# Two transformer blocks in one launch: another order for the passes of half the rows, the hyena's steps, norm and the bias loads

## The reference, cut to what matters

```python
logits = einsum('bqhd,bsd->bqhs', qib, k_idx32) * idx_scale      # 16 heads of 64; 2 blocks of 128 queries
score = einsum('bqhs,bqh->bqs', relu(logits), wb)                # then the 64 best keys of each query
...
h = h @ w4                                    # filter taps: 256 positions, 64 hidden, 2 x 1024 channels
h_fwd, h_bwd = h[:, :1024] * decay, h[:, 1024:] * decay
k = concatenate([h_fwd, zeros, h_bwd[:0:-1]])
k = k / sum(abs(k), axis=0)                   # "norm" in the kernel
...
z = hv * x1
z = bidir_fft_conv(z, filt) + hy_bias * z     # spectra of z and of the filter, product, back
y_h = z * x0
...
g_h, g_a = split(sigmoid(g + b_gate), 2)      # 8 groups of 512 columns
```

## Time and profile before

| | |
|---|---|
| median of 3 runs | 2093.49 us (2090.84 to 2102.37) |
| profiled execution | 2100.09 us, span 2098.3 us |
| mean granted clock of TensorE | 0.985 |
| TensorE busy | 97% |
| VectorE busy | 63% |
| ScalarE busy | 44% |
| DMA | 194 GB/s over the span |

### The profile page before, as it was taken

How to read it: one execution, slowest core, us unless ns; L and a number is a source line. 1 busy time by engine, 2 the same in 40 slices (tenths; PEclk the granted TensorE clock), 3 DMA queues, 4 the chain that set the end, 5 groups by cost and what they waited for, 6 DMA issues and landing times.

```text
span 2098.3 us, 23578 instructions
## 1 busy us (share of the span) xinstructions
PE 2043.2 (97%) x9229; PEld 1614.4 (77%) x9229; DVE 1317.6 (63%) x1675; ACT 927.6 (44%) x1226; POOL 382.9 (18%) x588
## 2 busy tenths in 40 slices
PE   6989999999999999999899999999999999999999
PEld 1268787777887888787688888888888888878887
DVE  4867667789676678867975665554444544444443
ACT  1165523455654544344454434454444444443342
POOL 0000001999999960000000000000000000000000
PEclk9999989999999999999999999999999999999999
DMA  9967656555566675544345555555555555656554
GB/s 351 331 246 240 212 185 207 189 177 161 178 199 196 197 228 180 178 142 157 124 150 177 198 186 179 184 195 184 197 181 195 185 193 188 198 163 200 189 192 160
DMA packets 206243, 407.94 MB, mean 194 GB/s; under 512 B 10874, under 2 KB 12979, under 8 KB 205491
## 3 DMA queue, kind: packets, MB, share of 16 engines
q1 hardware_dynamic: 190480, 376.07, 54.1%
q10 hardware_dynamic: 13892, 23.88, 3.4%
q0 software_dynamic: 1760, 6.49, 1.5%
HBM read 404.31 MB, written 2.10 MB: 194 GB/s over the span
## 4 chain that ended last, share of the span: by engine, by line
PE 88%; DVE 7%; DMA 3%; issue 1%; ACT 1%; ACTq 0%; SPq 0%; DVEq 0%
PE ps L430 80%; PE pm L511 5%; DMA raw<-in_ada_w 2%; DVE raw_lo L408 2%; PE ps L511 1%; PE pm L523 1%; DVE mod_part L1148 1%; DMA raw<-in_w_in 1%; PE pm L575 0%; PE pm L885 0%; DVE xtmp L1348 0%; DVE sc_i L1265 0%; DMA gate<-in_b_gate 0%; DVE xtmp L1546 0%; DMA rows_b<-in_hgrn_norm_g 0%
## 5 line engine op out<-in xcount | busy, mean ns | idle before, releaser
L408 DVE TENSOR_TENSOR raw_lo<-raw,w_hi 128x1024 fp32r<-128x1024 f32 (+1 forms) x648 | 799.5, 1237 | 580.0 <-ACT w_hi L399 570.6
L399 ACT ACTIVATE w_hi<-raw 128x1024 fp32r<-128x1024 f32 (+1 forms) x648 | 680.1, 1051 | 809.4 <-PE ps L430 783.5
L430 PE MATMUL ps<-w_hi,h_hi 128*128 128x512 f32 (+1 forms) x2336 | 943.8, 404 | 19.7 <-DVE raw_lo L408 13.5
L430 PE MATMUL ps<-w_hi,h_lo 128*128 128x512 f32 (+1 forms) x2336 | 915.1, 392 | 0.0
L430 PE MATMUL ps<-raw_lo,h_hi 128*128 128x512 f32 (+1 forms) x2336 | 914.7, 392 | 0.0
L430 PEld LDWEIGHTS ps<-w_hi,h_hi 128*128 128x128 f32 x2336 | 444.1, 190 | 126.6 <-DVE raw_lo L408 20.7
L430 PEld LDWEIGHTS ps<-raw_lo,h_hi 128*128 128x128 f32 x2336 | 444.6, 190 | 93.1 <-issue 7.4
L430 PEld LDWEIGHTS ps<-w_hi,h_lo 128*128 128x128 f32 x2336 | 443.8, 190 | 93.7
L2305 POOL TENSOR_TENSOR proj<-proj 128x128 f32<-128x128 f32 x264 | 177.0, 675 | 12.9
L2305 POOL TENSOR_TENSOR proj<-proj,w1T 128x128 f32<-128x128 f32 x165 | 102.3, 628 | 11.3 <-DMA proj<-in_z 4.1
L430 PE MATMUL ps<-w_hi,hid_hi 128*128 128x512 f32 x256 | 100.0, 391 | 2.0 <-DVE raw_lo L408 2.0
(11 more groups left out here) (320 smaller groups left out, 1168.0 us busy)
## 6 DMA issues: line engine op xcount, KB each, us to landing
raw<-in_w_in SPq DMA_DIRECT2D x140, 1024.0 KB, 5.3
raw<-in_w_ffn_gate SPq DMA_DIRECT2D x44, 1024.0 KB, 5.1
raw<-in_w_ffn_up SPq DMA_DIRECT2D x44, 1024.0 KB, 5.1
raw<-in_w_ffn_down SPq DMA_DIRECT2D x44, 1024.0 KB, 5.1
raw<-in_ada_w SPq DMA_DIRECT2D x32, 1024.0 KB, 7.7
raw<-in_w_out SPq DMA_DIRECT2D x32, 1024.0 KB, 5.2
proj<-in_ada_w ACTq DMA_DIRECT2D x16, 1024.0 KB, 5.2
raw<-in_w_br_hyena SPq DMA_DIRECT2D x8, 1024.0 KB, 5.2
```

The costliest lines, as they stand in the source:

```text
L399: nc.scalar.activation(w_hi[:, p % HRING, :, 0:gm.width(j)], raw[:, k % RING, e:e + HT, 0:gm.width(j)], ACT.Copy).then_inc(hi_done, 1)
L408: nc.vector.tensor_tensor(raw_lo[:, k % RING, e:e + HT, 0:gm.width(j)], raw[:, k % RING, e:e + HT, 0:gm.width(j)], w_hi[:, p % HRING, :, 0 ...
L430: mm = nc.tensor.matmul(ps[pair][:, t, 0:gm.width(j)], l[:, tok], r[:, i, 0:gm.width(j)], start=(k == 0 and q == 0), stop=(k == kt - 1 and ...
```

## The change

Index: the steps j and j+1 are done together at the part of the even one, in two banks, and the products alternate between the row halves. Taps: two units at a time, products alternate between row halves and banks. Norm: DVE adds `decay[:, 1]` to `decay[:, 0]` first, and TensorE does one product per block of channels. z's spectrum: the second four units are two parts later; DVE's twelve steps are done at most one a part (in parts 81, 83, and 84 to 93); the convolutions start at part 97. Bias: slot 0 is loaded after the weight loads of group 9, slot 1 after those of group 10.

```diff
@@ -96,7 +96,7 @@
 SPEC_AT = 69
 Z_AT = 56
 ZSPEC_AT = 77
-CONV_AT = 92
+CONV_AT = 97
 ROTATE_AT = 72
 QK2_AT = 86
 AT2_AT = 93
@@ -656,15 +656,17 @@
                 i.then_inc(filled, 1)
                 for t in range(TT):
                     nk = P * (t + 1)
-                    for j in range(IDX_H // 2):
+                    for j in range(0, IDX_H // 2, 2):
                         yield INDEX_AT[1 + t] + j
                         if t == 0 and j == 0:
                             drained(("ki", 0))
-                        b = bank(pe, ("ix", t, j), "a")
-                        part = slice(IDX_D * (j % 2), IDX_D * (j % 2) + IDX_D)
+                        b = [bank(pe, ("ix", t, j + r), "a") for r in range(2)]
                         for q in range(2):
-                            m = mm(b[:, q * SEQ:q * SEQ + nk], qiT[part, j // 2 * 2 + q, t * P:t * P + P], kiT[part, 0:nk])
-                        m.then_inc(filled, 1)
+                            for r in range(2):
+                                part = slice(IDX_D * r, IDX_D * r + IDX_D)
+                                m = mm(b[r][:, q * SEQ:q * SEQ + nk], qiT[part, j + q, t * P:t * P + P], kiT[part, 0:nk])
+                                if q:
+                                    m.then_inc(filled, 1)
 
             def gate_rows():
                 for j in range(ADA_GATE):
@@ -752,24 +754,23 @@
                     yield i2(LAYER_AT[n])
                     pe.wait_ge(sig(f"sin{n + 1}"), 1)
                     mm(bank(pe, ("layer", n), "v")[:, 0:P], w23[:, n], h3T[:]).then_inc(filled, 1)
-                for i in range(4 * TT):
-                    yield i2(TAPS_AT + i // 2)
-                    if i == 0:
+                for n in range(4):
+                    yield i2(TAPS_AT + n)
+                    if n == 0:
                         pe.wait_ge(sig("w4_in"), 16 * TT)
                         pe.wait_ge(sig("sin3"), 1)
-                    odd, n = i % TT, i // TT
-                    b = bank(pe, ("taps", odd, n), "v")
-                    for t in range(TT):
+                    b = [bank(pe, ("taps", odd, n), "v") for odd in range(2)]
+                    for odd, t in ((1, 0), (0, 1), (0, 0), (1, 1)):
                         part = slice(HID * t, HID * t + HID)
-                        m = mm(b[P // 2 * t:P // 2 * t + P // 2, :], h3T[part, :].rearrange("p (m s) -> p s m", s=2)[:, odd],
+                        m = mm(b[odd][P // 2 * t:P // 2 * t + P // 2, :], h3T[part, :].rearrange("p (m s) -> p s m", s=2)[:, odd],
                                w4[part, n * GW:n * GW + GW], skip_group_check=True)
-                    m.then_inc(filled, 1)
+                        if (odd, t) in ((0, 0), (1, 1)):
+                            m.then_inc(filled, 1)
                 yield i2(NORM_AT)
                 pe.wait_ge(sig("abs_ready"), 1)
                 b = bank(pe, "norm", "v")
                 for c in range(8):
-                    for t in range(TT):
-                        m = mm(b[:, c:c + 1], decay[:, t, c * P:c * P + P], ones[:, 0:1], start=(t == 0), stop=(t == TT - 1))
+                    m = mm(b[:, c:c + 1], decay[:, 0, c * P:c * P + P], ones[:, 0:1])
                 m.then_inc(filled, 1)
                 for i in range(8):
                     yield i2(SPEC_AT + i)
@@ -796,7 +797,7 @@
                             m = nc.tensor.transpose(b[:, c * P:c * P + P], y_t[4 * u + c].rearrange("p (m s) -> p s m", s=2)[:, t], ident[:])
                         m.then_inc(filled, 1)
                 for i in range(8):
-                    yield i2(ZSPEC_AT + i)
+                    yield i2(ZSPEC_AT + i + 2 * (i // 4))
                     drained(("z", 1, 1))
                     n, j, odd = i // 4, i // 2 % 2, i % 2
                     mm(bank(pe, ("zspec", n, j, odd), "v" if odd else "a")[:, :], dft[:, j, odd, 0:P],
@@ -1480,6 +1481,7 @@
                     yield i2(ABS_AT + 3 * t + 2)
                     link(v.tensor_tensor(decay[:, t], decay[:, t], w4v[:, t], ALU.add))
                     yield i2(ABS_AT + 3 * t + 3)
+                link(v.tensor_tensor(decay[:, 0], decay[:, 0], decay[:, 1], ALU.add))
                 dve.sem_inc(sig("abs_ready"), 1)
                 for t in range(TT):
                     link(v.tensor_tensor(w4v[:, t], hf[:, t], hb[:, t], ALU.subtract))
@@ -1562,10 +1564,10 @@
                         dve.sem_inc(sig("y_spec"), 1)
 
                 for at, step in ((1, lambda: slots(("zspec", 0, 0), hf, 0, 0)), (3, lambda: slots(("zspec", 0, 1), hb, 0, 1)),
-                                 (4, lambda: slot_product(0, 0)), (5, lambda: slots(("zspec", 1, 0), hf, 1, 0)),
-                                 (5, lambda: slot_product(0, 1)), (6, lambda: parities(0, 0)), (7, lambda: slots(("zspec", 1, 1), hb, 1, 1)),
-                                 (7, lambda: parities(0, 1)), (8, lambda: slot_product(1, 0)), (9, lambda: slot_product(1, 1)),
-                                 (10, lambda: parities(1, 0)), (11, lambda: parities(1, 1))):
+                                 (4, lambda: slot_product(0, 0)), (5, lambda: slot_product(0, 1)), (6, lambda: parities(0, 0)),
+                                 (7, lambda: slots(("zspec", 1, 0), hf, 1, 0)), (8, lambda: parities(0, 1)),
+                                 (9, lambda: slots(("zspec", 1, 1), hb, 1, 1)), (10, lambda: slot_product(1, 0)),
+                                 (11, lambda: slot_product(1, 1)), (12, lambda: parities(1, 0)), (13, lambda: parities(1, 1))):
                     yield i2(ZSPEC_AT + at + LEAD)
                     step()
                 for c in range(8):
@@ -2125,7 +2127,7 @@
                         turned_by(("x0", 3))
                         s.activation(z_tok[:, t, u * GW:u * GW + GW], b[:, :], ACT.Copy).then_inc(used["a"], 1)
                 for i in range(4):
-                    yield i2(ZSPEC_AT + 2 * i + LEAD)
+                    yield i2(ZSPEC_AT + 2 * i + 2 * (i // 2) + LEAD)
                     n, j = i // 2, i % 2
                     b = content(act, ("zspec", n, j, 0), "a")
                     s.activation((hf, hb)[j][:, 0, n * GW:n * GW + GW], b[:, :], ACT.Copy).then_inc(used["a"], 1)
@@ -2252,7 +2254,7 @@
 
             def beside_i2(j):
 
-                for g in (0, 1) if j == I2_G + 1 else (j - I2_G,) if j > I2_G + 1 else ():
+                for g in (j - I2_G,) if j >= I2_G else ():
                     if g >= 2:
                         evacuated(sp, g_i2, j - 2)
                     else:
```

## The result

The changed kernel takes 2082.76 us (median of 18 runs, 2080.76 to 2090.40); the kernel before, run beside it, 2096.81 (18 runs). The ratio is 0.9933, with a 95% interval of 0.9923 to 0.9943: faster by some 14 us, 0.67%. The forecast was a gain of 12.5 us and 2081.0 us. The profiled execution has a span of 2080.8 us and a mean granted clock of 0.987.

What follows compares the result with a forecast made beforehand. TensorE, busy 97% of the span, was taken as the bound. Index -2.0, taps 0, norm -3.5, convolutions 0, bias and steps -7.0 sum to -12.5 us: 2081.0 us on the median, range 2074 to 2090.

Steps and rivals of the forecast that it cites:

- Bound: Whole kernel: TensorE busy for 97% of the span, so edits pay by removing its instructions, waits or slow stretches.
- Index, -2.0 us: Paired index steps: passes overlap, relieving TensorE of 8.6 us, but VectorE covers them; 2.6 us gained, 0.6 off for slow clock.
- Taps, 0: Taps products alternating over row halves and banks: they overlap already, so no gain; range +1 to -4 us.
- Rival D: Taps: row halves in one bank wait for each other today, so separate banks save 3.9 us; 2077.1 us, chance 0.04.
- Norm, -3.5 us: Norm: 16 passes instead of 32 save 1.8 us, plus half of the 3.4 us lost to slow clock behind them.
- Bias and steps, -7.0 us: Hyena's steps: the bias stall goes and low halves come earlier; 7.8 us gained, 0.8 off for slow clock.
- Convolutions with attention, 0: Six parts instead of one fill all four banks: no cost entered, up to +6 us.
- Rival C: Parts 99 to 104: TensorE waits for readers of all four banks, costing 15 us; 2096 us, chance 0.06.
- The sum: All terms together: 12.5 us gained, giving 2081.0 us on the median.
- rival B: Waits in parts 86, 87 and before part 100 bring slow clock, norm's slow stretch stays: +6.8 us, 2087.8 us, chance 0.27.

Runs made afterwards that it cites:

- norm_only: The kernel before with the norm edit alone (added sum, one product per block): 2091.82 us, ratio 0.9987.
- bias_only: The kernel before with only the bias loads moved: 2089.05 us, ratio 0.9983.
- steps_only: The kernel before with only the later second spectrum units, VectorE's new list of steps and convolutions from part 97: 2090.46 us, ratio 0.9981.
- steps_wide: The changed kernel with the hyena's steps spread wider (VectorE's in parts 81 to 97) and convolutions from part 101: 2082.09 us, ratio to before 0.9939.
- q_later: The changed kernel with the second attention's transposes of q two parts later and of k one part later: 2084.59 us, ratio to before 0.9959.
- search_late: The changed kernel with the second row block's search for the 64 best keys one round a part from two parts later: 2085.40 us.
- index_only: The kernel before with the paired index steps alone: 2093.21 us, ratio 1.0001.
- both_moved: The changed kernel with the edits of both search_late and steps_wide: 2081.11 us, ratio to before 0.9935.
- both_mended: both_moved with convolutions from part 97 again and the first sine layer two parts later: 2076.94 us, ratio to before 0.9908.
- in_turn: The changed kernel with both index products of the lower row half issued first, still in two banks: 2089.76 us in one execution.
- norot pair: The kernel before without the first attention's rotations on VectorE, once with the index as before (2091.10 us), once with the index edit (2084.50 us).
- norot_single: The kernel before without the first attention's rotations on VectorE, index as before: 2091.10 us, ratio 0.9980.

## Why the prediction was right, and where it was off

**Bound.** Right: the gain is instructions and slow clock of TensorE, and the waits for low halves stayed at 14.6 us.

**Index, -2.0 us.** The mechanism held in each step: passes of 0.72 and 1.14 us, a wait near 452 us, VectorE as the cover (8.5 us arrive without its rotations), a gain that is VectorE's alone. The size was too large: 1.0 us in the trace of the changed kernel, 1.2 in that of the edit alone, nothing that shows in its ratio. Two terms were mis-sized. VectorE's starts came 2.0 us earlier, not 2.6. And I wrote off 0.6 us for slow clock, with the new wait before part 100 as its likely cause; it was a second one, the 3.04 us before 506.65, that had the slow stretch behind it, some 1.1 us lost (clock 0.91 over 500 to 520). I had taken the existing wait of 1.63 us there as something that stays as it is; it became 1.28 and 3.04, since TensorE arrived earlier and VectorE hardly did. That is the forecast's own rule, that an earlier TensorE waits longer, not carried to the end of the stretch.

**Taps, 0.** Right: eight passes in 1.94 us before and after the earlier trace rows. The rule of the Trainium skill that was weighed there (TensorEngine Tiling (Array Packing), Gotcha 1: PSUM Pressure) doesn't show where the halves write to different partitions of a bank: giving them a bank each changed nothing. Rival D has fallen.

**Norm, -3.5 us.** Too small: 5.0 us in the trace, close to the upper end of its range, 5.2. The 1.8 us of passes were right; the slow stretch behind them, of which I had taken half, went altogether (1.00 where 0.79 stood), in the changed kernel and in norm_only. bias_only keeps the 32 passes and had them in 3.62 us instead of 4.51, with a granted clock of 0.89 over the 16 us from their start, and gains 1.6 us on the kernel before there without any edit of norm: against that execution sixteen passes are worth 3.4 us. How much is slow varies from one execution to the next; that no slow stretch follows sixteen did not, in eight.

**Bias and steps, -7.0 us.** Right: 7.6, or 6.6 to 7.1 without what was chance in the execution before. The stall went, and the low halves of parts 83 to 93 came in the forecast's order. TensorE was to be idle for 5.3 us in pieces of 1.0 to 1.5; it was 4.3 in pieces of 0.96, 0.76, 1.35 and 1.22, two of them ahead of q's transposes as I had said (1.0 and 1.5), and the clock stayed at 1.00. That neither edit alone does it, and that about half comes from each, is what bias_only and steps_only add.

**Convolutions with attention, 0.** Right: TensorE busy for 70.00 of 70.00 us. Rival C didn't come, though steps_wide shows its mechanism in one part, 99, when the convolutions start four parts later still.

**The sum.** Two errors of opposite sign, index 1.0 too large and norm 1.5 too small, met, so 12.5 stood against 13.6 in the traces and 14.0 in the medians; that they nearly cancelled is luck. The time, 2082.76, lies 1.8 us above 2081.0: the kernel before took 2096.81 in the longer set of runs instead of 2093.49, 3.3 us more, and the gain was 1.5 us larger. None of rival B's slow stretches came in the changed kernel's trace; the one behind the wait near part 100 came in four other kernels (below). B was weighed by two waits, 1.63 us without a slow stretch and 3.75 with one. The same trace of before had more to weigh it by: a wait of 1.87 us at 1026 us and one of 2.22 at 641 were each followed by a slow stretch, one of 1.99 at 1851 was not.

## What to carry to other kernels

Count the work that an edit takes off the busiest engine, and then look for the engine that is ready just in time beside it: the index edit relieved TensorE of 8.5 us and brought about 1, because VectorE was busy 96% of the stretch. Where a second engine is without a pause, change its work or its order; and when that pays, look further down the program for the engine that the gain does not reach (GpSimd's filter sum here) and for the place whose cover was moved. Where VectorE set the pace, two waits of TensorE that were taken away came back as one longer one (q_later), with the same idle time in all and a slow stretch behind it.

## What the runs showed of the hardware that was not expected

**The same wait has two prices.** All kernels with the paired index passes have a wait of 1.85 to 1.90 us for a low half near 455 us. The 8 us behind it, in the changed kernel and in search_late, where nothing differs up to there:

```profile
451.98:459.98 8.00, 7.83 (x33) 5.99 (x34) 7.44 (x20) 2.12 (x2) 7.53 (x14) 1.00 0.43 139
```

```profile
456.15:464.15 8.00, 8.00 (x28) 6.45 (x29) 7.44 (x20) 1.68 (x2) 7.53 (x14) 0.79 0.31 118
```

The granted clock was 1.00 in four kernels (the changed one, index_only, both_moved, both_mended) and 0.79 in four (in_turn, q_later, search_late, steps_wide), which lose 1.2 us there. So about 1 us of difference between single executions is chance. A longer wait for VectorE, before some transposes near 636 us, shows the same in two kernels that do not differ up to there, bias_only first and then steps_only:

```profile
635.89 0.66 PE L710 MATMUL pm<-ident,proj 128*128 128x128 f32 x4 [2.33 <-DVEq L1329]
```

```profile
637.08 0.92 PE L710 MATMUL pm<-ident,proj 128*128 128x128 f32 x4 [2.33 <-DVEq L1329]
```

The granted clock over the 8 us from there was 1.00 in the first and 0.79 in the second. In the fourteen traces, from 300 us on, no wait of 1.21 to 1.71 us had slow passes right behind it, waits of 1.85 to 2.34 us had them or not, and all waits of 2.91 us and more had.

**One-column passes.** A pass of one column takes 0.11 us (16 in 1.84). Over the 16 us from the first of 32 such passes the granted clock was 0.79 in five kernels (before, index_only, steps_only and the norot pair) and 0.89 in bias_only; over the 16 us from the first of 16 it was 1.00 in all eight that have them.

**GpSimd beside VectorE.** A filter sum is always the same 51 operations on 128x128 elements, and GpSimd took longer for it where VectorE had more to do. The second sum behind 430 us, with its loads' two issues, in the kernel before and in norot_single, which leaves out VectorE's rotations beside it (third and fifth of the busy times are VectorE and GpSimd):

```profile
439.44:478.81 39.37, 39.37 (x172) 30.18 (x170) 37.22 (x65) 22.84 (x48) 36.72 (x53) 1.00 0.58 185
```

```profile
435.94:471.33 35.39, 35.39 (x155) 27.54 (x154) 26.12 (x50) 20.64 (x43) 32.73 (x53) 1.00 0.53 169
```

It took 39.4 to 39.7 us in the twelve kernels with the rotations, 35.4 and 36.3 in the two without. VectorE's share of busy time alone doesn't tell it: another sum of search_late took 34.9 us of GpSimd with VectorE 57% busy, and one took 30.9 with VectorE 72% busy. Which of VectorE's instructions slow GpSimd wasn't tried.
